# Moving sixteen modulation blocks of a two-block transformer kernel from three layer norms and the entry of block 2 to the end of the first mixer of block 2

## The reference, cut to what matters

```python
x = layer_norm(DN_ALPHA * x + mix, ln1_g[layer], ln1_b[layer])          # block 1, four of these
x = layer_norm(DN_ALPHA * x + sqrelu_mlp(x, mlp_w1[layer], mlp_w2[layer]), ...)

def modulation(cvec, w_mod, b_mod):                                      # block 2
    m = jax.nn.silu(cvec) @ w_mod + b_mod
    return jnp.split(m[:, None, :], N_MOD, axis=-1)
...
hl = modulate(rmsnorm(xl, g_pre_mix[i]), ml[0], ml[1])
y_l = mix_stream(...)
xl_new = xl + ml[2] * rmsnorm(y_l, g_post_mix[i])
h2 = modulate(rmsnorm(xl_new, g_pre_mlp[i]), ml[3], ml[4])
xl_new = xl_new + ml[5] * rmsnorm(sqrelu_mlp_2(h2, w_mlp_in[i], w_mlp_out[i]), g_post_mlp[i])
```

## Time and profile before

| What | Value |
|---|---|
| Median of three runs | 1869.27 us (1866.08 to 1869.99) |
| Profiled execution, its own time | 1873.77 us |
| Its span, first to last instruction | 1872.0 us |
| Mean granted TensorE clock | 0.953 |
| Busy PE, DVE, ACT, POOL | 90%, 66%, 26%, 25% |
| Transfers | 247.28 MB, mean 132 GB/s |

### The profile page before, as it was taken

One profiled execution on the slowest core, in us unless ns is written; L12 is line 12 of the kernel. 1 busy time (PEld: TensorE's weight loads), 2 busy tenths in 40 slices (PEclk: granted clock), 3 DMA queues, 4 the chain that ended last, 5 costly groups with the idle time before them and its releaser, 6 DMA issues.

```text
span 1872.0 us, 27006 instructions
## 1 busy us (share of the span) xinstructions
PE 1687.3 (90%) x10974; PEld 1450.7 (77%) x10974; DVE 1232.1 (66%) x1668; ACT 488.0 (26%) x1009; POOL 473.1 (25%) x368
## 2 busy tenths in 40 slices
PE   7888589999787899999988979999999788989997
PEld 6776479999687799998744748888888475679996
DVE  7752458887776788868874474444444696568886
ACT  3323222111350412222345351111011424541111
POOL 2300124443231444412200302121221130134442
PEclk9999799999898999999988989999999898999998
DMA  7445665555464655554200203233333141035551
GB/s 264 147 151 176 226 213 165 178 177 166 169 214 158 213 178 177 176 177 158 90 1 1 84 19 112 90 101 92 98 97 94 35 136 43 23 102 180 178 177 49
DMA packets 69876, 247.28 MB, mean 132 GB/s; under 512 B 7456, under 2 KB 10528, under 8 KB 69664
## 3 DMA queue, kind: packets, MB, share of 16 engines
q1 hardware_dynamic: 69792, 246.18, 40.2%
HBM read 245.10 MB, written 1.05 MB: 131 GB/s over the span
## 4 chain that ended last, share of the span: by engine, by line
PE 60%; DVE 29%; ACT 5%; issue 5%; POOL 1%; DMA 1%; SPq 0%; DVEq 0%; POOLq 0%; ACTq 0%
PE psum L319 13%; PE psum L321 12%; PE psum L320 12%; DVE lo_ring L294 9%; DVE relu L1125 4%; DVE hid_lo L1126 3%; PE psum L335 3%; PE psum L337 2%; PE psum L336 2%; PE psum L1449 2%; PE psum L953 2%; DVE c_conf L1678 2%; DVE x L1088 1%; PE psum L1473 1%; PE psum L409 1%
## 5 line engine op out<-in xcount | busy, mean ns | idle before, releaser
L1905 POOL TENSOR_SCALAR hi_ring<-raw_ring 128x1024 fp32r<-128x1024 f32 x364 | 472.9, 1302 | 1372.0 <-PE psum L321 675.4
L294 DVE TENSOR_TENSOR lo_ring<-raw_ring,hi_ring 128x1024 fp32r<-128x1024 f32 x364 | 542.4, 1492 | 92.8 <-POOL hi_ring L1905 59.8
L319 PE MATMUL psum<-x_hi,hi_ring 128*128 128x256 f32 (+1 forms) x1424 | 447.5, 314 | 22.6 <-DVE lo_ring L294 22.5
L320 PE MATMUL psum<-x_lo,hi_ring 128*128 128x256 f32 (+1 forms) x1424 | 442.1, 310 | 0.0
L321 PE MATMUL psum<-x_hi,lo_ring 128*128 128x256 f32 (+1 forms) x1424 | 441.7, 310 | 0.0
L319 PE MATMUL psum<-hid_hi,hi_ring 128*128 128x256 f32 (+1 forms) x1024 | 316.8, 309 | 4.2 <-DVE hid_lo L1126 4.2
L321 PE MATMUL psum<-hid_hi,lo_ring 128*128 128x256 f32 (+1 forms) x1024 | 315.0, 308 | 0.0
L320 PE MATMUL psum<-hid_lo,hi_ring 128*128 128x256 f32 (+1 forms) x1024 | 313.7, 306 | 0.0
L319 PEld LDWEIGHTS psum<-x_hi,hi_ring 128*128 128x128 f32 x1424 | 275.7, 194 | 41.9 <-DVE lo_ring L294 27.8
L320 PEld LDWEIGHTS psum<-x_lo,hi_ring 128*128 128x128 f32 x1424 | 275.7, 194 | 13.5 <-issue 0.2
L321 PEld LDWEIGHTS psum<-x_hi,lo_ring 128*128 128x128 f32 x1424 | 275.4, 193 | 13.2
(11 more groups left out here) (370 smaller groups left out, 1932.0 us busy)
## 6 DMA issues: line engine op xcount, KB each, us to landing
raw_ring<-weights SPq DMA_DIRECT2D x460, 512.0 KB, 4.0
h_const<-hyb_consts SPq DMA_DIRECT2D x1, 1088.0 KB, 11.6
x<-xT SPq DMA_DIRECT2D x1, 1024.0 KB, 5.8
x<-ctxT SPq DMA_DIRECT2D x1, 1024.0 KB, 17.1
outT<-x SPq DMA_DIRECT2D x1, 1024.0 KB, 4.8
shared<-shared_consts SPq DMA_DIRECT2D x1, 398.0 KB, 13.7
par<-params SPq DMA_DIRECT2D x1, 301.5 KB, 6.4
```

The costliest lines, as they stand in the source:

```text
L294: nc.vector.tensor_tensor(lo_ring[:, u % SPLIT_SLOTS, :], raw_ring[:, UNIT_AT[u] % RAW_SLOTS, :], hi_ring[:, u % SPLIT_SLOTS, :].bitcast(F ...
L319: nc.tensor.matmul(bank(u % BANKS, T), w_hi, hi[:, k, 0:T], start=(k == 0), stop=False)
L320: nc.tensor.matmul(bank(u % BANKS, T), w_hi, lo[:, k, 0:T], start=False, stop=False)
L1905: nc.gpsimd.tensor_scalar(hi_ring[:, u % SPLIT_SLOTS, :], raw_ring[:, slot, :], 1.0, 0.0, ALU.mult, ALU.add).then_inc(hi_ready, 1)
```

## The change

`_NORM` gives each of the three norms two "mean" and two "norm" mods where it gave two and six. The entry of block 2 gets two and six where it had four and eight. The sixteen mods so set free stand between the mixer and the MLP of layer 0 of block 2: twelve ("gated") behind the sum of the mixer's output, four ("pre_mlp") behind the sum for the MLP's input. `AFTER_MODS` loses the first units of both MLPs of block 1 and of the recurrent mixer, so that `next_lo` splits them at the end of the stage before. The batches become 14, 10, 16 and 8. The last batch is turned behind the first quarter of layer 0's MLP, for which this quarter is written out ahead of PE's loop, and its sums and the coefficients of layer 1 are made in the second quarter. ACT's copy of a batch's rows (L430) moves from behind the last block of a modulated norm to behind the chunk that begins with block 4.

```diff
-_NORM = lambda n: [(f"mean{n}", 2), (f"norm{n}", 6)]
+_NORM = lambda n: [(f"mean{n}", 2), (f"norm{n}", 2)]
-_STREAM += [MLP_UNITS, ("mean3", 4), EARLY, ("pre_mix", 8), L2_UNITS - EARLY, L2_UNITS]
+_STREAM += [MLP_UNITS, ("mean3", 2), EARLY, ("pre_mix", 6), L2_IN + 3 + KT - EARLY, ("gated", 12), ("pre_mlp", 4), MLP_UNITS, L2_UNITS]
...
-AFTER_MODS = {u + i for u in (U_HOUT, U_MLP1, U_REC, U_ROUT, U_MLP2) for i in range(LEAD)} | {U_L2 + LEAD}
+AFTER_MODS = {u + i for u in (U_HOUT, U_ROUT) for i in range(LEAD)} | {U_L2 + LEAD}
...
-BATCHES = [14, 10, 11, 13]
+BATCHES = [14, 10, 16, 8]
...
-    SUMS_TAKEN = [0, 2, 4]
+    SUMS_TAKEN = [0, 2, 3, 4]
...
-        if place:
-            next_mods_act(act, place)
+        if place and a == 4:
+            next_mods_act(act, place)
...
         if s is not None:
-            first_los(dve, ahead)
             dve.wait_ge(flag("norm_rstd"), n + 1)
...
+        first = 0
+        if m == 2:
+            quarter(0)
+            turn_batch(pe, 3)
+            first = 1
+        with pe.Fori(first, QUARTERS) as i:
+            quarter(i)
...
+            if m == 2 and i == 1:
+                take_sums(dve, 2)
+                coef_dve(dve, link, 1)
...
                 if l == 0:
-                    turn_batch(pe, 3)
+                    turn_batch(pe, 2)
...
                 norm_pe(pe, L.norm + 1, L.T)
+                if L.l == 0:
+                    mods(pe, "gated")
                 norm_pe(pe, L.norm + 2, L.T)
+                if L.l == 0:
+                    mods(pe, "pre_mlp")
```

More of the change, by code:

```diff
@@ L1093, in mlp_pe, with quarter @@
     def mlp_pe(pe, m, base, T, s):
-        with pe.Fori(0, QUARTERS) as i:
+        def quarter(i):
             turn = lambda u: i * 4 + u // BANKS
@@ L1935, in _ @@
                 norm_rstd_act(act, link, L.norm + 2, L.T, 1)
-                modulated_act(act, L.split + 2, L.T, L.l, 3)
+                modulated_act(act, L.split + 2, L.T, L.l, 3, None if L.l else "pre_mlp")
                 base = L.base + L2_IN + 3 + KT
@@ L1947, in _ @@
             hyb_dve(dve, link)
-            layer_norm_dve(dve, link, 0, 0, "ln1_g", "ln1_b", 0, U_MLP1)
+            layer_norm_dve(dve, link, 0, 0, "ln1_g", "ln1_b", 0, None)
             link(nc.vector.tensor_scalar(y[:, :, 0:SEQ], x[:, :, 0:SEQ], ALPHA, None, ALU.mult))
             mlp_dve(dve, link, 0, U_MLP1, SEQ)
-            layer_norm_dve(dve, link, 1, 1, "ln2_g", "ln2_b", 1, U_REC)
+            layer_norm_dve(dve, link, 1, 1, "ln2_g", "ln2_b", 1, None)
             rec_dve(dve, link, 1)
-            layer_norm_dve(dve, link, 2, 2, "ln1_g", "ln1_b", 3, U_MLP2)
+            layer_norm_dve(dve, link, 2, 2, "ln1_g", "ln1_b", 3, None)
             link(nc.vector.tensor_scalar(y[:, :, 0:SEQ], x[:, :, 0:SEQ], ALPHA, None, ALU.mult))
@@ L1959, in _ @@
                 l2_dve(dve, link, L)
-                if L.l == 0:
-                    coef_dve(dve, link, 1)
                 gated_dve(dve, link, L.norm + 1, L.T, L.l, 2)
```

## The result

| | before | after |
|---|---|---|
| median of 8 timed runs | 1869.55 us (1866.08 to 1873.61) | 1874.30 us (1872.97 to 1878.01) |
| ratio after / before | | 1.0028, 95% interval 1.0017 to 1.0038 |
| profiled execution: time, span | 1873.77, 1872.0 us | 1875.92, 1874.1 us |

The account below looks back on a forecast made before the run. Neither PE (60% of the span) nor DVE (29%) was taken to bound everywhere; the wait ending last in each stretch counts. -15.1 - 1.2 + 20.8 + 0.4 + 0.4 = +5.3 us gave 1874.6 us, range 1871.5 to 1876.5.

Parts of the forecast that it names:

- Norms: Norms 0 to 2: L1005 starts just behind `rstd` once splits move earlier; gain 5.30 + 5.61 + 4.23 = 15.1 us.
- the ring: At norm 0, units 30 to 33 could load only when mods 48 to 51 were done; POOL waited 17.98 us.
- What is late next at the norms: Behind norms 0 to 2, x itself comes late next, unchanged; a warm PE gains nothing.
- Rival 2: At the norms, less PE idling may keep the clock at 2.4 GHz: -8 us, net -2.8, 1866.5; chance 0.07.
- Entry of block 2: Two fewer mods in "mean3" and in "pre_mix": gain 1.2 us, between 0.9 and 1.6.
- The new place: End of layer 0's mixer: DVE stands at unit 211's split behind the mods; gated update 20.8 us later, 17.7 to 21.6.
- the hold: In the load burst behind the mixer's sums: an extra delay of about 1.2 us, inferred from the burst behind mean3.
- Small terms: Layer 0's MLP: turning the last batch about 0.4 us, ACT's copy of the rows +0.4 us, four "pre_mlp" mods nothing.
- The prediction's own test: Called wrong if the update follows `rstd` within 15 us, norms give under 4 us each, or the stretch between norms changes.
- 1: New place: shorter wait, no hold, splits at landing pace; 17.7 us for 20.8, +2.2 us, 1871.5; chance 0.22.
- 3: Norms gain less: moved splits wait for rounding, mean or y comes late, 1 to 2 us each; +9, 1878; chance 0.07.
- 4: New place: no DVE wait because the units' transfers pass the mods; -15.5, 1853.8; chance 0.02.

Follow-up runs that it names:

- E6: Changed kernel with DVE's three splits at norms 0 to 2 back between centring and L1005, four mods per norm kept; one run, 1874.89 us.
- E7: Changed kernel with five spare matmuls behind the mods of norms 0 and 1 to keep PE at work; one run, 1873.52 us.
- E3: Changed kernel with the first three units of layer 0's MLP behind the twelve "gated" mods but ahead of the four "pre_mlp"; 1868.85 us, 1.0002 of before.
- E10: E2 with five spare matmuls behind norm 0's mods alone; 1849.93 us, 0.9888 of before.
- E8: Changed kernel with 896 bytes left free ahead of y, restoring tile addresses modulo 1024 as before; 1875.76 us, 1.0047 of before.
- E2: Changed kernel with layer 0's first three MLP units ahead of the sixteen mods, split eight "gated" and eight "pre_mlp"; 1849.94 us, 0.9895 of before.
- E9: Kernel before, unedited, profiled once more for scatter; 1872.36 us.
- E5: Kernel before with WIDE set to 16, moving the tiles behind cond by 128 bytes; 1868.31 us, 1.0007 of before.
- E1: Changed kernel with layer 0's first three MLP units ahead of the sixteen mods, still twelve "gated" and four "pre_mlp"; 1856.23 us, 0.9938 of before.
- E4: Changed kernel, stream untouched, with DVE's splits of layer 0's first three MLP units behind the gated update; 1857.40 us, 0.9935 of before.
- E11: Changed kernel, unedited, profiled once more for scatter; 1875.68 us.

## Why the prediction was right, and where it was not

The sum was right (+5.3 forecast, +5.2 timed), and so was the mechanism of both of its large terms. That the total came out so close is partly luck: the terms that I named come to +7.4 us in the profile, stretches that I had called unchanged take 5.3 off, and the timed runs add 3 again.

**Norms.** 5.30 + 5.61 + 4.23 was forecast, 5.30, 5.62 and 4.23 is what the profile shows from centring to L1005; E6 shows that nearly all of it is the ring.

**What is late next at the norms: the failed step.** I wrote that "x ends the stretch and a warm PE gains nothing". That was true of the kernel before: at norm 2 ACT's relu came 1.44 us behind the last x_lo. A window of the changed kernel there (the third number from the end is the clock), and from its timelines DVE's last x_lo and ACT's relu:

```profile
610.00:612.00 2.00, 2.00 (x12) 2.00 (x11) 0.99 (x2) 1.88 (x5) 0.00 (x0) 0.50 0.17 68
```

```profile
611.47 0.69 DVE L999 TENSOR_TENSOR x_lo<-x,x_hi 128x512 fp32r<-128x512 f32 x1 [1.01 <-ACT x_hi L991]
...
615.08 0.38 ACT L1120 ACTIVATE relu<-psum 128x256 f32<-128x256 f32 x1 [2.90 <-PE psum L337]
```

Now it comes 2.92 us behind. x is ready 4.2 us sooner, but the clock falls later against x (from the clock of the two-microsecond windows at about 606.6, 3.1 us behind L1005; before at about 619.3, 0.6 us ahead of it), so the slow matmuls reach past the last x_lo and are no longer made good while PE waits for x. At norm 2 that gives back 1.5 of the 4.2 us: L1005 to relu takes 11.54 us against 10.05. At norm 0 it is 0.3 us against before, since x itself came 0.8 us slower there before; E7 shows that a warm PE would have gained 1.5. Rival 2 had the right resource and mostly the wrong sign: with less idle time the clock still fell at 23 of 27 norms, at a place where it costs; where it stayed up at norm 2 (E3), the 1.5 us were there. At norm 1 the sentence holds in E3 and E7; E10 is 1.7 us shorter there, but in it the fall near 518 of the other profiles is missing too.

**Entry of block 2.** -1.2 forecast with 0.9 as its bound, -0.86 measured.

**The new place.** 20.8 us forecast, 22.7 measured, outside the bound of 21.6 (which follows from none of the terms that I gave): both parts were too short, not the mechanism. The first issue came 0.6 us behind the sums (0.7 forecast). The first new mod was used 4.3 us behind the sums, the next two 2.67 and 2.19 us later instead of 1.26 each: the hold was 2.3 us and not 1.2. From the fourth (1067.79) five transfers took 6.4 us, 1.28 each where 1.26 was forecast. In E7, without the hold, unit 211 reaches POOL 14.6 us behind the sums and not 16.9 (15.7 forecast), and the wait is 20.4 us. Then POOL and DVE took 7.26 us from 1074.20 to 1081.46 where 6.5 was forecast. I counted three roundings and three splits; POOL's row shows that it rounds a fourth unit (x1 and x3), since the ring had gone on.

By the lock of the Trainium skill ("SBUF — State Buffer", section "SBUF: two separate sides") the three pairs gave 6.8 us. E3 has just three pairs and takes 6.4 us, nearer to the 6.5 of the forecast. In the changed kernel the fourth rounding ends at 1080.47, ahead of the last split's end, so all seven instructions lie inside the 7.26 us, where their lengths alone add up to 4 x 1.05 + 3 x 1.23 = 7.9. The trace agrees with the lock in that a rounding and a split beside each other both show about 2 us (2.01 and 1.98), where alone they show 1.05 and 1.23; that they take turns costs a little less than their lengths alone.

**Small terms.** ACT's copy +0.24 for 0.4, the turn 0.47 for 0.4 (E8 against before). The four "pre_mlp" mods cost nothing that can be seen; eight of them cost 0.7 (E2).

**The sum of these terms** as measured is -15.15 - 0.86 + 22.68 + 0.24 + 0.47 = +7.4 us in the profile, so 5.3 us of gain stand in stretches that I had called unchanged. 2.9 of them are what E8 gives back behind norm 0's centring: +3.25 in the 512-column MLP, -2.9 in the MLP behind norm 2, -2.45 behind layer 1's update, -0.8 elsewhere. The other 2.3 are -3.9 in the mixer, of which 1.6 is scatter (E9), and -1.3 in the MLP behind norm 0, against +1.5 for the cold clock at norm 2, +1.1 ahead of norm 0's centring and +0.3. The -1.3 is most likely the place of the tiles too: E8 has norm 0 warm and gains 1.5 us by it, which hides as much of what the place costs there (E5, which has the clock of before, is 3.0 us shorter than before in this stage). The centring of norm 0 stands at 260.5 to 262.9 us in the three profiles with the order of before and at 261.6 to 264.3 in the ten with the changed one (262.9 in E6, with the splits back), so whether the moved splits cost something ahead of it is not settled. The cause of the mixer's other 2.3 us stays open. So does why the timed runs of before lie 4.2 us under its first profile and those of the changed kernel 1.6: my step from a profile to a median was a guess that held. The prediction's own test, "if the stretch between the norms changes its length", came out against it, although the total did not.

**Rivals.** 1 (17.7 us of wait) is refuted by 22.7. One half of it, a burst without the hold, came true in E7, with 20.4 us; the other half, splits at the pace of landing, in no run. 3 is refuted at the norms by E6 (only ahead of norm 0's centring a part of it stays open), 4 by POOL's wait for the transfer, and 2 by the clock, which fell at all three norms of the changed kernel.

## What to carry to other kernels

In a ring that loads in order, ask of each block of filler work which queue already holds a consumer of what comes behind it: sixteen mods ahead of the next stage's weights cost 22 us of wait, behind them 3.9 (E1) or 0.7 (E2). The order of the stream undoes the wait, and that of the waiting engine's queue undoes 15.7 us of it (E4). Put ahead of a reduction only as much filler as the ring already holds (E2). When a wait in front of a stage goes, look again at PE's clock in the first matmuls behind it, since "the slow ones are made good while waiting" holds only as long as there is a wait.

## What the runs showed of the hardware

- The start-to-start time of 512-column matmuls depends on where the moving tile lies: 0.229 us each with `hid_hi` and `hid_lo` at their old places or 1024 bytes from there, 0.233 with them 128 bytes further. The matmuls that read `x_hi`, whose place did not move, keep their time. With 256 columns the sign was the other way, 0.118 us each at the old places and 0.1135 to 0.1145 at the new ones, 1 to 3 us per MLP. Whole stages show it less steadily: in E11 the one behind norm 0 moved by 0.6 us with no edit.
- A burst of loads that starts on idle queues can hold behind the first transfer: 4.86 us for the second and third together in the changed kernel, 2.6 in E7, and 1.28 us each from the fourth on in both. The nine profiles with a hold have a 16 KB transfer of instructions about 1 us behind the sums and a late third issue of SP, E7 has neither.
- Five spare matmuls of 256 columns, 2.4 us of work into an unused bank of PSUM, went with a granted clock of 1.00 at norms 0 and 1 (3 of 3). Without them it fell to 0.50 for 6.8 us at 14 of 17 such norms of the changed order.
